# Head of a two-layer hybrid decoder step in a new order: filler products on TensorE, later powers, norms pair by pair

## The chip, the cores and the metric

One core of a Trainium2 chip. The time is that of one execution of the whole program on the device, in microseconds (us), and the result is the median of several executions. The engines are PE (TensorE, the matrix engine), DVE (VectorE), ACT (ScalarE), POOL (GpSimd) and SP (SyncE, which here only starts DMAs). They run side by side, each through its own instruction list, and meet through semaphores.

## The reference

Two layers over 256 prompt tokens and 64 sample tokens, 320 columns in all, 1024 features:

```python
for l in range(DEPTH):                                    # DEPTH = 2
    mod = silu(c) @ w_ada + b_ada                         # c: one prompt and 8 sample conditions
    shift, scale, gate = split(mod, 3)
    h = rms_norm(x, norm_g) * (1 + scale) + shift
    q, k, v, za, u, zs = split(h @ w_in)
    ya = attend(rope(q), rope(k), v, sinks)               # window 128
    ys, state = s5_branch(u, ...)                         # complex diagonal SSM, gelu, GLU
    x = x + gate * (concat(ya * silu(za), ys * silu(zs)) @ w_out)
y = rms_norm(x, final_g)
```

`s5_branch` needs, from small parameters only, `exp(a*dt)` with its sines and cosines, its powers 1 to 8 and B scaled by a coefficient. New key and value windows and SSM states are outputs too. All is float32.

## The kernel before, in words

Every engine's instruction list is written out by hand; nothing is scheduled by a planner. Activations lie feature by token: `xT`, eight tiles of 128x320. A dense product with a 1024x128 block of weights is made in three passes of float32r, `h_hi*w_hi + h_lo*w_hi + h_hi*w_lo`: ACT copies the block to `w_hi` (`hi_part`), DVE subtracts for `w_lo` (`lo_part`), and two buffers of each (`HL = 2`) are in use by turns. `DENSE` lists the blocks: u0 to u3, q0 to q3, k, v, za, zs, glu, out. PE's `project` makes 16 products of the high part and then 8 of the low part; `project_two` does u0 and u1 tile by tile, since it follows the tiles of `h` as they come.

**The head (layer 0).** SP starts the loads: condition, 16 half-megabyte blocks of `w_ada` (ss0 to ss15), small parameters, `ssm_b`, u0 and u1 and the rest. PE turns the condition, then x (eight tiles `xT0` to `xT7`); ACT squares each tile (`first_rows`, L1223), DVE copies it (L1619), and sums of squares go through `first_squares` and `newton` to `rstd`, which `spread_root` lays over all rows (`rb`). `modulation(0, "ssN")` multiplies block N with the condition: 2 products of 512 columns that use a quarter of the array's columns each. After four blocks ACT copies the sum (`modulation_rows`, L1288), PE turns it (`turn_modulation`, L798), and DVE adds it up to shift and scale (`modulation_of`, L1718 to L1726). Blocks 0 to 7 give shift and scale for tiles 0 to 3 of `h`, blocks 8 to 15 those for tiles 4 to 7. For a pair of tiles ACT scales and shifts the prompt's columns (L1323), DVE the samples' (L1899, L1902), ACT rounds to `h_hi` (L1328) and DVE subtracts for `h_lo` (L1906).

Between these lies the preparation of the SSM: DVE makes the angles and denominators (L1664 to L1679), ACT one Exp and two Sin (L1264, L1257, L1258), DVE the first power and the coefficient (`powers`), then `higher_powers`, `inputs_scaled` (B), `wide_powers`, and four times `turned_inputs`, whose results PE turns (`turn_B`, L862, placed by `TURNED_AFTER`). `lo_part(0, 2)` to `lo_part(0, 5)` stand among these on DVE, and `lo_part(0, 6)`, for q2, behind `outputs_summed` and `carriers(0, 0)`.

**The boundary.** While layer 0's out0 to out7 are added to x, ACT squares each tile into one of two buffers `sq`, DVE adds the first seven to `sqsum` (`add_square`), and PE sums over rows (`sum_squares`). At the start of layer 1 DVE scales tiles 0 to 3 by `rb` (`normed`, L1871) before the first pair, and 4 to 7 before the third.

PSUM's eight banks are three rings (`proj` 2 banks, `ada` 1, `work` 5), and a job of a ring waits until the job before it in its bank is read.

## Time and profile before

| | |
|---|---|
| median of 3 runs | 403.86 us (399.94 to 405.77) |
| profiled execution, time | 400.8 us |
| its span | 399.0 us |
| mean granted clock of TensorE | 0.97 of full speed |
| PE, DVE, ACT, POOL busy | 359.9, 316.1, 197.2, 64.8 us |
| DMA | 72.27 MB, mean 181 GB/s |

Times in rows are microseconds from the span's start. A row of the timeline has start, duration (from the first start to the last end where several are merged), engine, line, operation, `out<-in`, rows and columns, the count of records, and in brackets how long the engine sat idle before it and what it waited for.
### The profile page before, as it was taken

The page shows a single profiled execution, that of the slowest core. Times are in us where ns is not written, and L with a number is a line of the kernel's source. Part 1 is how long each engine was busy: PE and PEld are TensorE (multiplying, and loading weights), DVE is VectorE, ACT ScalarE, POOL GpSimd, SP SyncE. Part 2 cuts the span into 40 slices and gives each one's busy share as a digit, 9 for nine tenths or more (in the row PEclk, how much of TensorE's full clock was granted, in tenths as well). Part 3 has the DMA queues.
Part 4 walks back from the last instruction along what each step waited for, and adds up shares of the span by engine and source line. Part 5 has one row for each costly group of instructions (what it writes and reads, how often), then busy time and mean ns, then how long its engine had stood idle before and what let it go on. Part 6 is the DMA issues. An engine that isn't in the chain of part 4 may idle for free. (4 is left out here: it accounts for less than half of the span.)

```text
span 399.0 us, 8243 instructions
## 1 busy us (share of the span) xinstructions
PE 359.9 (90%) x3122; PEld 313.2 (79%) x3122; DVE 316.1 (79%) x676; ACT 197.2 (49%) x423; POOL 64.8 (16%) x58
## 2 busy tenths in 40 slices
PE   0997589998999799999999759999999999899993
PEld 0462379987979597977989758999997988779992
DVE  1648889977899958898599876889699589976863
ACT  2365255365463117787335556427633177863432
POOL 3200000020000370000499800000000000002430
PEclk9999969999999899999999959999999999999998
DMA  8999826799839966953995072391998279522303
GB/s 247 292 349 369 203 60 229 244 169 204 264 101 267 268 176 168 352 125 92 294 301 103 2 235 67 91 167 46 287 176 214 45 202 334 142 64 59 100 2 131
DMA packets 125125, 72.27 MB, mean 181 GB/s; under 512 B 63385, under 2 KB 111605, under 8 KB 124990
## 3 DMA queue, kind: packets, MB, share of 16 engines
q1 hardware_dynamic: 111118, 65.05, 61.3%
q10 hardware_dynamic: 13968, 6.69, 7.3%
q8 instruction: 25, 0.41, 0.4%
q14 instruction: 14, 0.11, 0.1%
HBM read 64.74 MB, written 6.59 MB: 179 GB/s over the span
## 5 line engine op out<-in xcount | busy, mean ns | idle before, releaser
L691 PE MATMUL bank<-h_hi,w_hi 128*128 128x320 f32 x448 | 138.6, 322 | 13.0 <-DVE h_lo L1906 10.7
L691 PE MATMUL bank<-h_lo,w_hi 128*128 128x320 f32 x448 | 134.4, 312 | 0.0
L691 PEld LDWEIGHTS bank<-h_hi,w_hi 128*128 128x128 f32 x448 | 85.6, 191 | 21.0 <-issue 12.4
L691 PEld LDWEIGHTS bank<-h_lo,w_hi 128*128 128x128 f32 x448 | 85.7, 191 | 0.2
L691 PE MATMUL bank<-h_hi,w_lo 128*128 128x320 f32 x448 | 81.8, 312 | 0.0
L1702 DVE TENSOR_TENSOR w_lo<-raw,w_hi 128x1024 fp32r<-128x1024 f32 x50 | 63.0, 1259 | 10.7 <-ACT w_hi L1272 10.4
L691 PEld LDWEIGHTS bank<-h_hi,w_lo 128*128 128x128 f32 x448 | 70.9, 191 | 0.0
L1272 ACT ACTIVATE w_hi<-raw 128x1024 fp32r<-128x1024 f32 x50 | 52.7, 1053 | 31.0 <-DMA raw<-in_w_in 16.9
L2304 POOL TENSOR_TENSOR ga<-xT,fing 128x320 f32<-128x320 f32 x4 | 6.5, 1632 | 141.8 <-DVE xT L2185 141.8
L1452 ACT ACTIVATE R<-R,sm 128x128 f32<-128x128 f32 (+2 forms) x40 | 17.7, 443 | 9.6 <-issue 5.7
L691 PE MATMUL bank<-R,Gm 128*128 128x96 f32 x128 | 17.4, 297 | 3.8 <-DVE R L2039 3.8
L691 PEld LDWEIGHTS bank<-R,Gm 128*128 128x128 f32 x128 | 16.4, 209 | 4.4 <-DVE R L2039 4.2
L691 PE MATMUL bank<-R,cT 128*32 128x512 f32 x136 | 19.1, 613 | 0.0
L1567 ACT ACTIVATE ez<-xT 128x320 f32<-128x320 f32 x16 | 7.6, 472 | 22.8 <-DVE xT L2185 22.8
L1353 ACT ACTIVATE hn<-bank 128x320 f32<-128x320 f32 x12 | 5.3, 438 | 27.5 <-PE bank L691 14.5
L691 PE MATMUL bank<-U,R 128*128 128x96 f32 x128 | 14.9, 276 | 1.4 <-DMA U<-u_turn 1.0
L691 PEld LDWEIGHTS bank<-U,R 128*128 128x128 f32 x128 | 14.6, 192 | 1.9 <-DMA U<-u_turn 1.3
L2054 DVE TENSOR_TENSOR R<-bank,const 128x512 f32<-128x512 f32 (+1 forms) x16 | 9.7, 650 | 8.0 <-PE bank L691 8.0
L1412 ACT ACTIVATE ez<-bank 128x320 f32<-128x320 f32 x16 | 6.9, 431 | 15.6 <-PE bank L691 11.4
L1462 ACT ACTIVATE HY<-bank 128x320 f32<-128x320 f32 x8 | 3.4, 438 | 19.9 <-PE bank L691 19.7
L1650 DVE TENSOR_TENSOR sqsum<-sqsum,ez 128x320 f32<-128x320 f32 x12 | 12.9, 1073 | 0.0
L2289 POOL TENSOR_TENSOR R<-Asd,Bbar 128x512 f32<-128x512 f32 x4 | 5.3, 1316 | 45.7 <-DVE h_lo L2174 45.5
(321 smaller groups left out, 638.1 us busy)
## 6 DMA issues: line engine op xcount, KB each, us to landing
R<-in_w_ada SPq DMA_DIRECT2D x34, 512.0 KB, 6.6
raw<-in_w_in SPq DMA_DIRECT2D x32, 256.0 KB, 5.9
raw<-in_w_in SPq DMA_DIRECT2D x14, 512.0 KB, 6.2
raw<-in_w_out SPq DMA_DIRECT2D x32, 128.0 KB, 3.6
raw<-in_w_out SPq DMA_DIRECT2D x16, 256.0 KB, 4.0
raw<-in_w_ada SPq DMA_DIRECT2D x4, 512.0 KB, 8.2
R<-in_w_in SPq DMA_DIRECT2D x4, 512.0 KB, 11.4
raw<-in_w_glu SPq DMA_DIRECT2D x4, 512.0 KB, 4.4
```

What stands on the lines that cost most here:

```text
L691: return nc.tensor.matmul(out_, lhsT, rhs, start=start, stop=stop, skip_group_check=free)
L1272: fn(w_hi[:, n % HL, :], place(l, unit), ACT.Copy).then_inc(hi_done, 1)
L1353: fn(qraw[:, n % 2, :], proj.bank(l, job)[:, 0:TOK], ACT.Copy).then_inc(proj.emptied(l, job), 1)
L1412: fn(ez[:, n % 2, :], proj.bank(l, job)[:, 0:TOK], ACT.Tanh, scale=0.5).then_inc(gate_tanh, 1)
L1452: fn(buf[:, v, i, :], buf[:, v, i, :], ACT.Exp, scale=SCALE, bias=sm[:, g, 1, x:x + 1], accum_out=sm[:, g, 2, x:x + 1])
L1462: fn(Ysb[:, 8 * n:8 * n + 8, :].rearrange("p (q h) j -> p q (h j)", h=2), src, ACT.Copy)\
L1567: fn(sq[:, m % 2, :], xT[:, m, :], ACT.Square).then_inc(sq_done, 1)
L1650: tt(sqsum[:, :], sqsum[:, :], sq[:, n % 2, :], ALU.add).then_inc(sq_added, 1)
L1702: tt(w_lo[:, n % HL, :], place(l, unit), w_hi[:, n % HL, :].bitcast(F32), ALU.subtract)\
L2054: tt(dst, src, mask, ALU.add).then_inc(work.emptied(l, job), 1)
L2289: step.add(tt(im, A(Asd[:, 0]), B(Bbar[:, 0]), ALU.mult))
L2304: tt(xn(k), xT[:, k, :], fing[:, k:k + 1].to_broadcast([P, TOK]), ALU.mult).then_inc(yn_ready, 1)
```

## The change

- **Filler.** A new helper `stay_busy(bank, n, cols)` multiplies the constant tile `mean` with itself into a bank that is written anew afterwards: 12 such products of 128 columns before the condition is turned, 5 between that and x.
- **Loads.** The small parameters go ahead of ss0 and ss1. `ssm_b` goes behind ss11, u0 and u1 behind ss7.
- **PE in the head.** `turn_inputs_B` goes from behind the squares to behind `project_two`, and into the ring `work`. The tiles of `project_two` come ahead: the pair 0, 1 stands ahead of ss8 and the pair 2, 3 ahead of ss10, where they stood behind ss11 and ss13.
- **DVE in the head.** Denominators behind `newton`; angles and `powers` behind tiles 0 to 3 of `h`; `higher_powers` behind tile 7; `wide_powers` behind the last `turned_inputs`. A third pair sum of squares on DVE saves a third of the products in `first_squares`.
- **ACT in the head.** Both copies of the modulation ahead of `hi_part(0, 0)`; the Exp joins the Sins, behind the third copy; `inputs_B` behind u0.
- **After u3.** `TURNED_AFTER` puts WB0 and WB1 behind u3, WB2 and WB3 behind q0, WB4 and WB5 behind q1, WB6 and WB7 behind q2.
- **Boundary.** The sixth addition to `sqsum` is gone, and PE multiplies the tiles 6 and 7 from both `sq` buffers (12 products for 8, here and at the end). `normed` goes pair by pair.

On PE, between the squares and the first products of u0 and u1, before (`qT`, `kcT`, `Toep`, `R` hold ss4 to ss7, `pt` and `scan` ss8 and ss9, `Gm` ss10 to ss12; L798 turns a modulation):

```order
L691 MATMUL bank<-kcT,cT 32x512 x2
L798 MATMUL bank<-const,R 128x128 x4
L691 MATMUL bank<-Toep,cT 32x512 x2
L691 MATMUL bank<-R,cT 32x512 x2
L798 MATMUL bank<-const,R 128x128 x4
L691 MATMUL bank<-pt,cT 32x512 x2
L691 MATMUL bank<-scan,cT 32x512 x2
L691 MATMUL bank<-Gm,cT 32x512 x4
L691 MATMUL bank<-h_hi,w_hi 128x320
```

And now, at the same place:

```order
L689 MATMUL bank<-qT,cT 32x512 x2
L689 MATMUL bank<-const,rstd 128x128 x2
L689 MATMUL bank<-const,rstd 128x64
L805 MATMUL bank<-const,R 128x128 x4
L689 MATMUL bank<-kcT,cT 32x512 x2
L689 MATMUL bank<-Toep,cT 32x512 x2
L689 MATMUL bank<-R,cT 32x512 x2
L805 MATMUL bank<-const,R 128x128 x4
L689 MATMUL bank<-h_hi,w_hi 128x320
```

Behind the second turned modulation comes `h` at once, and the blocks ss8 to ss11 stand behind the twelve products that follow.

On ACT, from the copy of the second modulation to the last pair of `h`, before (L1288 copies a modulation, L1257 and L1258 are the Sins):

```order
L1257 ACT_TABLE_LOAD
L1257 ACTIVATE HY<-HY 128x32
L1258 ACTIVATE HY<-HY 128x32
L1272 ACTIVATE w_hi<-R 128x1024
L1288 ACTIVATE R<-bank 128x512
L1272 ACTIVATE w_hi<-R 128x1024
L1323 ACTIVATE hf<-ga,mod 128x256 x2
L1328 ACTIVATE h_hi<-hf 128x320 x2
```

And now, around the third and fourth copy of a modulation (L1293):

```order
L1333 ACTIVATE h_hi<-hf 128x320 x2
L1293 ACTIVATE R<-bank 128x512
L1264 ACT_TABLE_LOAD
L1264 ACTIVATE HY<-HY 128x32
L1265 ACT_TABLE_LOAD
L1265 ACTIVATE HY<-HY 128x32
L1266 ACTIVATE HY<-HY 128x32
L1293 ACTIVATE R<-bank 128x512
L1328 ACTIVATE hf<-gs,mod 128x256 x2
```

The sines have moved from in front of the first pair of `h` to between the second and the third, with one more table load.

On DVE, from the last pair of `h` on, before (L1802 begins `inputs_scaled`):

```order
L1899 TENSOR_TENSOR hf<-gs,mod 128x64 x2
L1902 TENSOR_TENSOR hf<-hf,mod 128x64 x2
L1906 TENSOR_TENSOR h_lo<-hf,h_hi 128x320 x2
L1802 TENSOR_TENSOR scan<-Bsb,coef 128x256
L1803 TENSOR_TENSOR scan<-Bsb,coef 128x256
L1804 TENSOR_TENSOR Bbar<-scan 128x256
```

And now (L1778 to L1784 are `higher_powers`, 21 instructions):

```order
L1915 TENSOR_TENSOR hf<-gs,mod 128x64 x2
L1918 TENSOR_TENSOR hf<-hf,mod 128x64 x2
L1922 TENSOR_TENSOR h_lo<-hf,h_hi 128x320 x2
L1778 TENSOR_TENSOR HY<-Apow 128x32
L1779 TENSOR_TENSOR HY<-Apow 128x32
L1780 TENSOR_TENSOR Apow<-HY 128x2x16
```

The powers stand between the last tile of `h` and all that prepares u2 to q2.

The core of the diff:

```diff
-TURNED_AFTER = ({"u3": (0, 1, 2, 3), "q0": (4, 5), "q1": (6,), "q2": (7,)},
+TURNED_AFTER = ({"u3": (0, 1), "q0": (2, 3), "q1": (4, 5), "q2": (6, 7)},
...
@@ SP
-            for m in range(2):
-                load(0, f"ss{m}")
             for name, r0, r1 in (("norm_g", R_G, R_BADA), ("b_ada", R_BADA, R_BGLU), ("b_glu", R_BGLU, R_D)):
...
-            for m in range(2, 6):
+            for m in range(8):
+                load(0, f"ss{m}")
+            sp.wait_ge(*work.ready(0, "cT"))
+            load(0, "u0")
+            load(0, "u1")
+            for m in range(8, 12):
                 load(0, f"ss{m}")
             for r, name in enumerate(("ssm_b_re", "ssm_b_im")):
...
@@ PE
+            def stay_busy(bank, n, cols=512):
+
+                for _ in range(n):
+                    mm(bank[:, 0:cols], mean[:, :], (const if cols > P else mean)[:, 0:cols], True, True)
+
+            pe.wait_ge(mean_set, 1)
+            b = work.bank(0, "cT")
+            stay_busy(b, 12, P)
             pe.wait_ge(const_in, 16)
             pe.wait_ge(silu_r, 1)
...
+            stay_busy(work.bank(0, "xT0"), 5, P)
             pe.wait_ge(x_in, 32)
...
                     mm(o, sqsum[:, toks], mean[:, 0:1], True, False)
-                    mm(o, xn(4)[:, toks], mean[:, 0:1], False, False)
-                    ins = mm(o, xn(6)[:, toks], mean[:, 0:1], False, True)
+                    ins = mm(o, xn(4)[:, toks], mean[:, 0:1], False, True)
...
                     mm(o, sqsum[:, toks], mean[:, 0:1], True, False)
+                    mm(o, sq[:, 0, toks], mean[:, 0:1], False, False)
                     ins = mm(o, sq[:, 1, toks], mean[:, 0:1], False, True)
...
                     first_squares()
-                    turn_inputs_B()
-                    for m in range(2, 4):
+                    for m in range(2, 5):
                         modulation(0, f"ss{m}")
                     spread_root(0)
-                    for m in range(4, 8):
+                    turn_modulation(0, 0)
+                    for m in range(5, 8):
                         modulation(0, f"ss{m}")
-                        if m == 5:
-                            turn_modulation(0, 0)
                     turn_modulation(0, 1)
-                    for m in range(8, 12):
-                        modulation(0, f"ss{m}")
                     project_two(0, ("u0", "u1"), range(2), True)
-                    turn_modulation(0, 2)
-                    for m in range(12, 14):
+                    for m in range(8, 10):
                         modulation(0, f"ss{m}")
                     project_two(0, ("u0", "u1"), range(2, 4), True)
-                    for m in range(14, 16):
+                    for m in range(10, 12):
+                        modulation(0, f"ss{m}")
+                    turn_modulation(0, 2)
+                    for m in range(12, 16):
                         modulation(0, f"ss{m}")
                     turn_modulation(0, 3)
                     project_two(0, ("u0", "u1"), range(4, KT), False)
+                    turn_inputs_B()
                     turn_inputs_C()
...
@@ ACT
                 if l == 0:
-                    inputs_B()
                     modulation_rows(0, 0)
-                    ssm_sines()
+                    modulation_rows(0, 1)
                     hi_part(0, 0)
-                    modulation_rows(0, 1)
                     hi_part(0, 1)
                 for pair in range(0, KT, 2):
-                    if l == 0 and pair in (2, 4):
-                        modulation_rows(0, 2 if pair == 2 else 3)
+                    if l == 0 and pair == 4:
+                        modulation_rows(0, 2)
+                        ssm_sines()
+                        modulation_rows(0, 3)
...
@@ DVE
                 if l == 0:
-                    powers()
+                    denominators()
...
-                else:
-                    normed(range(4))
                 for pair in range(0, KT, 2):
-                    if pair == 4:
+                    if l:
+                        normed((pair, pair + 1))
+                    elif pair == 4:
+                        angles()
                         normed(range(4, KT))
                         if l == 0:
-                            higher_powers()
+                            powers()
                             modulation_of(0, 2)
                             modulation_of(0, 3)
...
                 if l == 0:
+                    higher_powers()
+                    lo_part(0, 2)
                     inputs_scaled()
+                    for m in range(4):
+                        if m:
+                            lo_part(0, m + 2)
+                        turned_inputs(m)
                     wide_powers()
-                    for m in range(4):
-                        lo_part(0, m + 2)
-                        turned_inputs(m)
...
-                    if m:
+                    if 0 < m < KT - 1:
                         add_square(m - 1, (l + 1) * KT + m)
```

## Rows read from the trace of the kernel before

**Rows 1.** The page: TensorE's granted clock in 40 equal slices, in tenths.
```profile
PEclk9999969999999899999999959999999999999998
```

**Rows 2.** The chain that ended last, in order of time: start, us, what.
```profile
242.40 0.50 DVE h_lo L1906
...
389.59 1.39 PE bank L691 x16
```

**Rows 3.** Timeline of PE in the head.
```profile
6.06 0.99 PE L698 MATMUL bank<-const,R 9*128 9x9 f32 x8 [6.06 <-DVE R L1613]
9.99 3.73 PE L713 MATMUL bank<-const,R 128*128 128x128 f32 x12 [2.94 <-DMA R<-in_x_sample]
...
17.60 1.93 PE L691 MATMUL bank<-raw,cT 128*32 128x512 f32 x8
...
23.08 2.04 PE L723 MATMUL bank<-const,R 64*128 64x64 f32 x16
...
26.92 1.84 PE L691 MATMUL bank<-const,rstd 128*128 128x128 f32 x6
...
35.75 1.04 PE L691 MATMUL bank<-Gm,cT 128*32 128x512 f32 x8
38.73 0.38 PE L691 MATMUL bank<-h_hi,w_hi 128*128 128x320 f32 x1 [1.94 <-DVE h_lo L1906]
...
51.01 0.64 PE L691 MATMUL bank<-h_hi,w_hi 128*128 128x320 f32 x1 [4.51 <-DVE h_lo L1906]
...
57.99 3.71 PE L691 MATMUL bank<-const,Gm 128*64 128x128 f32 x64
```

**Rows 4.** Busy us (and records) of stretches, then PEclk, DMA share, GB/s.
```profile
50.70:54.10 3.40, 2.73 (x9) 2.33 (x10) 2.66 (x10) 2.01 (x5) 0.00 (x0) 0.50 0.16 27
...
136.00:139.40 3.40, 3.40 (x18) 3.40 (x18) 3.33 (x5) 0.60 (x2) 3.24 (x5) 0.51 1.13 337
```

**Rows 5.** Timeline of DVE, head and the stretch behind it.
```profile
29.37 0.22 DVE L1739 TENSOR_TENSOR Apow<-HY 128x32 f32<-128x32 f32 x1 [3.94 <-ACT HY L1258]
...
31.94 1.68 DVE L1871 TENSOR_TENSOR ga<-xT,bank 128x320 f32<-128x320 f32 x4
...
42.67 0.22 DVE L1763 TENSOR_TENSOR HY<-Apow 128x32 f32<-128x32 f32 x1
...
47.73 0.31 DVE L1718 TENSOR_REDUCE mod<-bank 128x36 f32<-128x144 f32 x1
...
53.60 0.42 DVE L1802 TENSOR_TENSOR scan<-Bsb,coef 128x256 f32<-128x256 f32 x1
...
82.19 1.23 DVE L1702 TENSOR_TENSOR w_lo<-raw,w_hi 128x1024 fp32r<-128x1024 f32 x1
```

**Rows 6.** Timeline of ACT in the head.
```profile
27.70 1.28 ACT L1257 ACT_TABLE_LOAD   x1
28.99 0.23 ACT L1257 ACTIVATE HY<-HY 128x32 f32<-128x32 f32 x1
...
33.63 0.60 ACT L1288 ACTIVATE R<-bank 128x512 f32<-128x512 f32 x1 [3.34 <-PE bank L691]
34.12 1.05 ACT L1272 ACTIVATE w_hi<-R 128x1024 fp32r<-128x1024 f32 x1
```

**Rows 7.** DMA of ss15: its issue on SP's timeline.
```profile
27.40 0.48 SPq L530 DMA_DIRECT2D u_sb<-in_w_ada  x1
```

**Rows 8.** DMA issues: count, KB each, us to landing.
```profile
u_sb<-in_w_ada SPq DMA_DIRECT2D x1, 512.0 KB, 11.1
```

**Rows 9.** Timeline of PE, later in layer 0.
```profile
84.10 1.34 PE L691 MATMUL bank<-h_hi,w_lo 128*128 128x320 f32 x8
...
130.96 1.71 PE L691 MATMUL bank<-kT,qT 64*128 64x128 f32 x16
135.58 5.44 PE L691 MATMUL bank<-R,Gm 128*128 128x96 f32 x32 [2.91 <-DVE R L2039]
```

**Rows 10.** Timeline of DVE at the start of layer 1.
```profile
231.91 1.68 DVE L1871 TENSOR_TENSOR ga<-xT,bank 128x320 f32<-128x320 f32 x4 [1.93 <-PE bank L691]
```

More of the change, by code:

```diff
@@ L643, in _ @@
                     .then_inc(b_in, 16)
-            for m in range(6, 8):
-                load(0, f"ss{m}")
-            sp.wait_ge(*work.ready(0, "cT"))
-            load(0, "u0")
-            load(0, "u1")
-            for m in range(8, 16):
+            for m in range(12, 16):
                 load(0, f"ss{m}")
```

73 lines of the change are left out of this document (40 added, 33 removed).

## The prediction

> **What bounds the kernel now.** I read the page first, for where PE stands still and for its clock, then the chain of waits, then PE's timeline in the head, and last DVE's and ACT's at the same times. The page shows a clock near full speed but for four dips [rows 1], and from its busy shares PE as the main engine. The chain shows how much of this change can count: its tail passes through the last `h_lo` of layer 1 and the 16 records of the last sum of squares [rows 2]. So both boundary edits stand on the path, and what the head gains must come through PE to the end of layer 0.
>
> In the head PE has two losses. Equal products, four of 512 columns, take 1.93 us at 17.60 and 1.04 us at 35.75 [rows 3]: in the head the clock is at its lower level (1.2 GHz), and from some 34 us on at 2.4 GHz. And PE waits for `h`: 1.94 us before the first pair, 4.51 us before the third, and after this idle its 320-column products start at 0.64 us where they started at 0.38: the lower level again [rows 3], granted 0.50 in that stretch though PE is busy for 2.73 of 3.4 us [rows 4]. Behind the head PE hardly waits. One place matters: q2's low pass starts at 84.10 [rows 9], and DVE's `w_lo` for it ends at 82.19 + 1.23 = 83.4 [rows 5]. DVE is only 0.7 us ahead there.
>
> **Filler.** Eight products of 128 columns take 1.71 us late in layer 0, at the upper level [rows 9]: 0.21 each, so 0.43 at the lower. The other near row has three for 1.84 us at the lower level [rows 3], 0.61 each. Twelve cost 5.1 to 7.4 us from 1.0 on. I take 5.1, since constant tiles are nearer to the first row: they end at 6.2, and the condition, turned at 6.06 before [rows 3], loses nothing. It ends at 7.2, five more end at 9.4. x was there at 9.99 with a megabyte of ss0 and ss1 queued beside it [rows 3]; now it comes earlier. So x starts at 9.4, and at 12.9 by the dearer price.
>
> Their gain is the clock. What the profile shows of a rise is mixed: products of 96 columns without a gap run from 135.58, the stretch 136.0 to 139.4 still stands at 0.51, and the slices behind it are full again [rows 1, 4, 9]; but 7.6 us of turned x from 9.99 on brought none [rows 3]. The Trainium skill (TensorE: Matmul & The Clock Gate, "What's actually happening") says that the default state is throttled and that activity releases it. By that rule alone the turned x would have released it too; in this trace it did not, and the measurement decides. The filler is like what ran before the rise at 139.4, not like turned tiles, so I take it that it lifts the clock.
>
> **To the first pair of h.** Before, x takes 9.99 to 17.60 and the rest to the second modulation's copy lasts until 33.63 [rows 3, 6]. At the upper level PE stops being the pace of x; ACT's and DVE's copies are. I take 6.7 us, between PE's half (3.8) and the old 7.6, near the upper end since DVE has a dozen small steps in between: the squares start at 16.1. Of the 16.0 us behind 17.60 the turn of B (2.04, [rows 3]) and a third of the squares (about 1.2) leave, and ss4 to ss7 in other groups cost about 1.6, as blocks that use the same quarter of columns can't run side by side: 14.4, at the upper level 7.2, less 1.0 for ss0 and ss1, which now fit under x. The copy of the second modulation is at 22.4 instead of 33.63. From there to the first product was 38.73 - 33.63 = 5.1; the first high part (1.05, [rows 6]) now stands behind this copy, so 6.15: the first pair at 28.6, ten earlier. ss7, u0 and u1 have landed by then, since `ssm_b` went behind them.
>
> **To the third pair.** PE now has nothing between 23.5 and 28.6, where ss8 to ss11 stood. As behind the 4.51 us, I expect the lower level afterwards. Twenty-four products of h took from 51.01 to 57.99 less 0.4 of waiting, nearly all at the lower level, 6.5 us, and four blocks take twice 1.86: 10.2, or 5.3 at the upper level with twice 0.95 [rows 3]. The level comes back on the way, and I take the middle, 7.8: ss11 is done at 36.4. Then a chain that was spread out before: ACT's copy (0.6), two table loads of 1.28 and three small ones of 0.23 [rows 6], together 3.9 with the steps between: 40.3. DVE's `powers`, 31.94 - 29.37 = 2.6 [rows 5]: 42.9. From the start of the two last modulations to the end of the last pair 53.60 - 47.73 = 5.9 [rows 5]: 48.8. **The last pair ends at 48.8 instead of 53.6: 4.8 earlier.** Loads would allow 46.2: ss15 lands at 27.40 + 11.1 = 38.5 [rows 7, 8], plus product, copy and turn (about 2.2), one reduction less (0.4) and 5.9. By ACT's own row the next step starts 0.01 us after a table load [rows 6]; the Trainium skill (ScalarE: Activation LUTs, "What ACT_TABLE_LOAD costs") adds a drain and comes to 2.66 us each. With it the last pair would end 2.8 us later. The row shows none, so it stays out.
>
> **Where the gain goes.** `higher_powers` cost 47.73 - 42.67 = 5.1 us on DVE, and stood where PE waited for ss15 anyway. Now they stand behind the last pair, ahead of everything that feeds u2 to q2. `wide_powers` only changes its place within that stretch. So from the last pair to the part for q2 DVE needs 82.19 - 53.60 + 5.1 = 33.7 us: 48.8 + 33.7 = 82.5, ready at 83.7. PE would be there at about 79.9 (84.10 less 4.8, plus 1.0 for B's turn and less 0.4 for a turned tile that comes later); it waits 4 us and goes on at 83.7. **The 4.8 has become 0.4.** The later places of `TURNED_AFTER` spare PE a wait for the turned B, not this one. q3 and k follow one behind another from there; the scan on DVE, for which PE waits 2.91 at 135.58 [rows 9], has no free time to catch up, so the 0.4 stays.
>
> **Boundary and tail.** The chain's last sum of squares is 16 records in 1.39 us [rows 2]; with 24 it is 0.6 longer, and the addition saved ran beside ACT's last square: +0.6 at the end. At the first boundary copies on ACT cover it. Pair by pair the first tiles come 0.8 earlier (half of 1.68, [rows 10]), but DVE is the pace from 231.91 to 242.40 [rows 2, 10] and does the same work: +0.2. The new idle of 4 us before q2's low pass can cost clock: behind the 2.91 a stretch of 3.4 us stood at 0.51 [rows 4], 1.7 us; at three in ten that is +0.5.
>
> Sum: -0.4 + 0.6 + 0.2 + 0.5 = +0.9 on the profiled 400.8, so 401.7. The median of the runs shown is 3.1 above the profiled one; I put the forecast 0.4 under that offset, since one of its dips, behind 135.58, may fall otherwise: **404.3 us**.
>
> **Rivals.**
> - *The clock stays low in the head* (slower). If twelve fillers do not raise it, x ends at 17.0, squares at 21.4, the second copy is at 31.5 and the first pair at 37.7. Now ss8 to ss11 stand behind it, where they were done before: ss11 at 45.6, and the same chain of 12.4 gives 58.0 for the last pair: 4.4 later than before, with 5.1 of powers still behind. That is 9.2 above my case: 413.5. It decides where the level at the first modulation blocks is still that of 1.93 us for four products. For it: in the whole head before, it took until some 34 us. Against it: what ran ahead of the rise at 139.4 was such a stretch.
> - *The clock rises, and falls again at the squares*, for whose last sum PE waits after ss0 and ss1 as it now runs ahead of DVE: half of that, 407 to 410.
> - *The chain behind ss11 is covered.* If the clock holds over the gap before h, ss11 is at 33.9 and the last pair at the loads' 46.3: 2.5 less, 401.8; with waits that go elsewhere 399 to 402. Against it is the fall behind 4.51 us.
> - *More than that*, below 395.8, would need DVE to have spare time before q2; the 0.7 us speak against it.
> - *The gain doesn't arise at all* because loads bound the head: then the first pair stays near 38 while the clock is up; it ends near the second rival.
>
> The Trainium skill's same section on the clock makes idle time what throttles. By that rule the change works against itself, as it opens the gap before h; the fall behind the 4.51 us agrees, and the first case already carries it.
>
> **How the numbers follow.** Main case 0.48 (402 to 406.5), low clock 0.17, rise and fall 0.17, covered chain 0.14, more 0.04. The second case takes in loads that bound the head. The range leaves out the farthest gain and the top of the low-clock case, whose fillers could cost 3.5 more: 399.5 to 414. Two in a hundred, 8.1 us, is about what a measurement here tells from nothing: faster only in the last case and a bit of the one before, 0.05; slower in most of the low-clock case, 0.14; within, 0.81.
>
> **What would show it.** Right: four 512-column products near 1.0 us at ss0; a first pair of h near 28.6 and the last one's end near 49; two table loads before `powers`; PE idle some 4 us ahead of q2's low pass, put down to DVE's `w_lo`; 24 records at the end. Wrong: 1.9 us for those four products, or no idle before q2.

## The result and the profile after

The changed kernel takes **415.0 us** (median of 4, 413.3 to 420.8), the kernel before in the same session 402.8 (399.9 to 405.8): ratio 1.029, interval 1.018 to 1.040. Timed again with 6 executions it gave 414.9 and 1.031 (1.026 to 1.036). It is some 12 us slower, where 404.3 was forecast. The ratios leave out executions more than 1.5% above the fastest of their kernel; where over half of them lie there (`sinks_copy_early`, `changed_busy`), I go by the median of all.

The profiled execution is 413.5 us with a span of 411.7 and a mean granted clock of 0.929 (before: 400.8, 399.0, 0.970). The page's clock row, against [rows 1], has become restless in the first fifth:

```profile
PEclk9878779989999698999999869999998899999996
```

PE's timeline in the head, after:

```profile
1.06 4.67 PE L689 MATMUL bank<-mean 128*128 128x128 f32 x24 [1.06 <-DVE epsb L1615]
6.03 0.63 PE L703 MATMUL bank<-const,R 9*128 9x9 f32 x8 [0.29 <-DVE R L1620]
6.58 1.38 PE L689 MATMUL bank<-mean 128*128 128x128 f32 x10
8.57 2.35 PE L719 MATMUL bank<-const,R 128*128 128x128 f32 x12 [0.60 <-DMA R<-in_x_sample]
...
13.30 1.06 PE L689 MATMUL bank<-raw,cT 128*32 128x512 f32 x8
15.78 0.35 PE L689 MATMUL bank<-mean,sqsum 128*128 128x1 f32 x2 [1.42 <-DVE gs L1649]
...
17.07 1.06 PE L689 MATMUL bank<-raw,cT 128*32 128x512 f32 x8
18.88 1.92 PE L689 MATMUL bank<-qT,cT 128*32 128x512 f32 x4 [0.74 <-ACT R L1293]
...
26.95 0.66 PE L805 MATMUL bank<-const,R 128*128 128x128 f32 x4 [0.70 <-ACT R L1293]
32.63 0.60 PE L689 MATMUL bank<-h_hi,w_hi 128*128 128x320 f32 x1 [5.02 <-DVE h_lo L1922]
...
49.61 0.64 PE L689 MATMUL bank<-h_hi,w_hi 128*128 128x320 f32 x1 [4.69 <-DVE h_lo L1922]
...
82.01 2.50 PE L689 MATMUL bank<-R,cT 128*32 128x512 f32 x16 [3.63 <-DVE small L1935]
```

Read it by the price of equal work. Four products of 512 columns (x8) take 1.06 us at 13.30 and 17.07: the filler did lift the clock to 2.4 GHz, where [rows 3] had 1.93 us. At 18.88 two such products (x4) take 1.92: the level has fallen to 1.2 GHz, behind the wait of 1.42 us and the one-column products. So the first pair of `h` comes at 32.63. Windows over the stretches show the level (columns: busy time of PE, its weight loads, DVE, ACT and POOL, granted clock, DMA share, GB/s):

```profile
5.80:15.00 9.20, 7.74 (x52) 4.76 (x52) 5.32 (x16) 4.64 (x10) 2.67 (x3) 1.00 1.01 349
18.50:25.00 6.50, 6.12 (x22) 2.72 (x24) 2.73 (x9) 0.33 (x1) 0.00 (x0) 0.50 1.09 380
25.30:31.80 6.50, 1.61 (x12) 0.46 (x6) 3.61 (x9) 3.90 (x6) 0.95 (x1) 1.00 1.04 293
46.00:55.50 9.50, 5.76 (x20) 5.36 (x21) 7.67 (x35) 5.01 (x10) 0.00 (x0) 0.50 0.52 98
83.40:86.40 3.00, 3.00 (x14) 1.46 (x7) 2.93 (x5) 0.08 (x1) 1.62 (x2) 0.50 1.53 137
315.50:321.90 6.40, 6.40 (x31) 6.40 (x32) 6.30 (x11) 0.00 (x0) 0.00 (x0) 0.50 0.01 3
```

Note the second and third row: PE works for 6.12 of 6.5 us at 1.2 GHz, and idles for most of the next stretch at 2.4. The level follows what went before. DVE's timeline, against [rows 5]:

```profile
43.76 0.22 DVE L1754 TENSOR_TENSOR Apow<-HY 128x32 f32<-128x32 f32 x1 [4.24 <-ACT HY L1266]
...
51.16 0.89 DVE L1922 TENSOR_TENSOR h_lo<-hf,h_hi 128x320 fp32r<-128x320 f32 x2 [0.48 <-ACT h_hi L1333]
51.97 0.21 DVE L1778 TENSOR_TENSOR HY<-Apow 128x32 f32<-128x32 f32 x1
...
59.14 0.43 DVE L1817 TENSOR_TENSOR scan<-Bsb,coef 128x256 f32<-128x256 f32 x1 [0.90 <-ACT Bsb L1239]
...
81.80 0.15 DVE L1935 COPY small<-bank 128x4 f32<-128x4 f32 x1
...
86.53 2.36 DVE L1717 TENSOR_TENSOR w_lo<-raw,w_hi 128x1024 fp32r<-128x1024 f32 x2
```

The last pair ends at 52.05, 1.6 earlier than before; `w_lo` for q2 starts at 86.53 instead of 82.19, 4.3 later. Matching equal PE records of the two traces one by one shows where the end moved. The last column is after less before:

| place (PE) | before | after | difference |
|---|---|---|---|
| a product of u0 and u1, fourth pair | 55.11 | 53.47 | -1.6 |
| first product of u2 | 61.95 | 62.30 | +0.35 |
| first modulation of layer 1 | 78.83 | 82.01 | +3.2 |
| state products, layer 0 | 92.14 | 96.65 | +4.5 |
| products of the carried states (`R,Gm`), layer 0, record 22 of 64 | 139.63 | 143.94 | +4.3 |
| squares of layer 0, the second products with `sqsum` | 226.72 | 232.78 | +6.1 |
| carried states, layer 1, first record | 306.69 | 315.29 | +8.6 |
| carried states, layer 1, last of the first 32 records | 310.23 | 322.01 | +11.8 |
| last squares, the products of 64 columns | 390.54 | 402.96 | +12.4 |

Three places: the head (4.5), the scan of layer 1 (some 5, a wait of 2.62 us for 0.92 and 6.8 us at the lower level behind it), and bits between. The two rows of the scan, before and after:

```profile
306.69 3.81 PE L691 MATMUL bank<-R,Gm 128*128 128x96 f32 x32 [0.92 <-DVE R L2039]
```

```profile
315.29 7.06 PE L689 MATMUL bank<-R,Gm 128*128 128x96 f32 x32 [2.62 <-DVE R L2058]
```

The execution profiled before took 400.8 us where the median is 403.9. Matched in the same way against a second profile of that program (before_again below, span 404.1), the changed kernel is 2.7 us behind in the second half of the state products (3.9 there against the first profile) and only 1.8 behind just before the scan of layer 1 (6.8), and the scan costs 5.0 again. So the scan's part stands in both comparisons, while 5 of the 6.8 us in front of it are no more than two executions of one program differ by.

The chain of waits shows the scan's part, and the tail with 24 records where [rows 2] had 16:

```profile
295.33 0.60 SPq L536
295.98 8.29 DMA raw<-in_w_in
304.28 1.07 ACT w_hi L1277
305.38 1.23 DVE w_lo L1717
...
315.29 19.25 PE bank L689 x365
...
401.56 2.07 PE bank L689 x24
```

A weight load takes 8.29 us to land, ACT's `w_hi` waits for it, and DVE's `w_lo` and scan behind it.

### The profile page after: what moved, and what is told of

It reads as the page before. It is cut to its first block and busy times, and to the rows that moved or that the text cites. A ratio compares the mean times of both kernels' runs of the same rounds, so it can differ in the third digit from the quotient of the medians.

```text
span 411.7 us, 8326 instructions
## 1 busy us (share of the span) xinstructions
PE 370.9 (90%) x3164; PEld 325.5 (79%) x3164; DVE 315.2 (77%) x675; ACT 199.0 (48%) x424; POOL 64.7 (16%) x58
## 5 line engine op out<-in xcount | busy, mean ns | idle before, releaser
L689 PE MATMUL bank<-h_hi,w_hi 128*128 128x320 f32 x448 | 140.5, 326 | 16.0 <-DVE h_lo L1922 13.8
L689 PE MATMUL bank<-h_lo,w_hi 128*128 128x320 f32 x448 | 135.8, 315 | 0.0
L689 PEld LDWEIGHTS bank<-h_hi,w_hi 128*128 128x128 f32 x448 | 87.0, 194 | 23.7 <-issue 13.6
L689 PEld LDWEIGHTS bank<-h_lo,w_hi 128*128 128x128 f32 x448 | 87.2, 195 | 0.2
L689 PE MATMUL bank<-R,Gm 128*128 128x96 f32 x128 | 21.5, 343 | 5.5 <-DVE R L2058 5.5
L689 PEld LDWEIGHTS bank<-R,Gm 128*128 128x128 f32 x128 | 20.5, 254 | 6.1 <-DVE R L2058 5.9
L1360 ACT ACTIVATE hn<-bank 128x320 f32<-128x320 f32 x12 | 5.3, 438 | 28.7 <-PE bank L689 19.8
L2258 POOL MEMSET R<- 64x1280 f32 x4 | 4.6, 1160 | 58.4 <-PE bank L689 58.2
L689 PEld LDWEIGHTS bank<-R,cT 128*32 128x32 f32 x136 | 3.9, 110 | 12.5 <-issue 7.1
```

The lines of the kernel that those rows point to most:

```text
L689: return nc.tensor.matmul(out_, lhsT, rhs, start=start, stop=stop, skip_group_check=free)
L1360: fn(qraw[:, n % 2, :], proj.bank(l, job)[:, 0:TOK], ACT.Copy).then_inc(proj.emptied(l, job), 1)
L2258: nc.gpsimd.memset(Hblk[h * NST:(h + 1) * NST, :, :, 1 - h, :], 0.0).then_inc(hblk_zero, 1)
```

## The experiments

Eighteen kernels. Each was timed in turn with the kernel before; "of all" is the plain median of this kernel, "ratio" its time over that of the kernel before. The two do not always give the same difference, and where that matters both are given. The last four columns are from each one's profile: start of the first product of `h`, end of the last `h_lo` of layer 0, start of `w_lo` for q2, and PE's wait for R at the scan of layer 1.

| kernel | of all | ratio | interval | first h | last pair | w_lo q2 | R wait |
|---|---|---|---|---|---|---|---|
| before | 403.9 | | | 38.7 | 53.7 | 82.2 | 0.92 |
| before_again | 403.6 | 0.998 | 0.995-1.001 | 39.8 | 54.7 | 83.3 | 0.88 |
| changed_again | 414.9 | 1.031 | 1.026-1.036 | 33.6 | 54.5 | 88.3 | 2.67 |
| sinks_copy_early | 416.5 | 1.024 | 1.015-1.033 | 34.4 | 54.0 | 89.4 | 2.69 |
| boundary_of_before | 412.4 | 1.024 | 1.019-1.028 | 33.9 | 53.6 | 88.2 | 1.89 |
| boundary_alone | 406.3 | 1.008 | 1.004-1.011 | 38.2 | 53.2 | 81.7 | 1.12 |
| powers_early | 412.6 | 1.017 | 1.012-1.021 | 35.2 | 53.0 | 87.3 | 2.65 |
| higher_powers_back | 420.6 | 1.036 | 1.031-1.041 | 34.3 | 60.2 | 94.7 | 2.59 |
| changed_no_filler | 414.3 | 1.025 | 1.021-1.029 | 36.5 | 57.3 | 91.0 | 1.83 |
| before_with_filler | 407.4 | 1.009 | 1.005-1.012 | 38.4 | 53.4 | 81.9 | 2.62 |
| skews_late | 409.6 | 1.013 | 1.010-1.016 | 32.0 | 52.9 | 86.7 | 1.04 |
| all_early | 406.6 | 1.011 | 1.006-1.016 | 34.4 | 55.4 | 83.9 | 2.64 |
| all_early_no_fill | 406.7 | 1.006 | 1.004-1.009 | 36.4 | 57.8 | 86.3 | 1.03 |
| tiny_filler | 405.5 | 1.004 | 0.999-1.008 | 38.7 | 53.7 | 82.2 | 1.69 |
| before_skews_late | 402.2 | 0.993 | 0.990-0.996 | 38.6 | 53.5 | 82.0 | 0.94 |
| best_fill | 404.6 | 0.998 | 0.993-1.002 | 34.8 | 55.4 | 83.9 | 1.54 |
| best_fill_ss | 405.0 | 1.000 | 0.996-1.004 | 33.9 | 54.2 | 82.7 | 0.89 |
| changed_busy | 409.9 | 1.005 | 0.999-1.010 | 29.4 | 47.5 | 81.6 | 2.49 |
| best_busy | 406.0 | 1.005 | 1.000-1.009 | 31.7 | 51.9 | 80.4 | 1.19 |

**Both kernels once more.** Nothing edited.

> The changed kernel, nothing edited, for a second profile. In the first profiled execution it was 12.7 us longer than the kernel before: matched record by record, 3.9 of them stand at 100 us, 5.4 come at the scan of layer 1 (a wait of 2.6 us for R instead of 0.9, then a stretch at the lower clock), 1.2 at a dip near 158, the rest at the boundary and the tail. Theory 'head': only the wait ahead of layer 1's first modulation and what follows to 100 us belong to the change with certainty; the dips at 158 and 315 fall by chance. Then this profile has the wait of 3.6 us at 82 again, but other dips later, and the median is some 407 to 411 (before 402.8). Rival 'whole': the change sets the later dips too, through the times at which DMA and DVE work falls; then the dip behind the scan of layer 1 is there again, and the median is 412 to 416.

> The kernel before, nothing edited, for a second profile. All kernels profiled so far but two show a wait of 1.8 to 2.7 us for R at the scan of layer 1 (near 313) and the lower clock behind it, worth some 3 to 5 us; the first profile of the kernel before has 0.92 there and no fall. Theory 'chance': that was a lucky execution (400.8 beside a median of 403.3 to 404.1), and this one shows 1.8 or more with a span of 401 to 403. Theory 'head': the old head keeps DVE and its loads ahead, the wait is 0.9 again, and the gap of some 3.8 us that the new head loses behind 100 us is real.

Measured: the wait of 3.61 us at 83.8 is back, and so is all the rest: 2.67 at the scan of layer 1, median 414.9. The kernel before has 0.88 at its scan in a second profile:

```profile
311.73 0.69 PE L691 MATMUL bank<-R,Gm 128*128 128x96 f32 x4 [0.88 <-DVE R L2039]
```

So "chance" is out for that wait, though not for all falls of the clock: before_again, with a span of 404.1, has one at 155.9 to 159.3 that the first profile of the same program lacks.

**The wait at 82.** DVE's copy moved two turned inputs earlier.

```diff
                         turned_inputs(m)
+                        if m == 1:
+                            dve.wait_ge(sinks_turned, 1)
+                            dve.wait_ge(sinks_in, 48)
+                            cp(small[:, :, S_SINKS:S_SINKS + KV], ...)
                     wide_powers()
-                    dve.wait_ge(sinks_turned, 1)
-                    ...
```

> The changed kernel with DVE's copy of the sinks put behind the second turned input instead of behind the fourth and the wide powers. Theory 'ring': PE waits 3.63 us at 82.01 for this copy, since the bank that it empties takes the first modulation of layer 1, and falls to the lower clock behind the wait. With the copy at about 73 the wait goes; the modulation starts at about 78.4. But q2's low pass still waits for its w_lo at 86.5 + 1.2, so the wait only moves there: 2.0 to 3.5 us shorter in total than the changed kernel. Rival 'DVE': the wait is that of DVE's whole backlog, and moves entirely to w_lo: within 1 us of the changed kernel, with a wait of 3 us or more in front of q2's low pass.

The copy starts at 72.4 and the modulation waits for nothing, but q2's low pass does:

```profile
80.38 1.92 PE L689 MATMUL bank<-R,cT 128*32 128x512 f32 x16
...
90.67 1.70 PE L689 MATMUL bank<-h_hi,w_lo 128*128 128x320 f32 x5 [4.42 <-DVE w_lo L1717]
```

The rival holds in its mechanism: the wait is DVE's backlog, and the bank is only where PE meets it first. The times (416.5 of all, ratio 1.024) do not tell whether a microsecond was won.

**The boundary, both ways.** Squares of all tiles added on DVE and 8 and 16 products again, `normed` over four tiles; and the kernel before with those edits alone.

> The changed kernel with both layer boundaries as they were: squares summed on DVE for all eight tiles, 8 and 16 products instead of 12 and 24, the first four tiles normed together. Matched record by record, the changed kernel loses 0.8 us between the squares and the second pair of h of layer 1 and 0.9 at the tail. Theory 'small': 1.7 us shorter than the changed kernel, in those two places. Rival 'the boundary carries over': the later start of layer 1's first pairs moves the scan of layer 1 and its dip as well: 5 us shorter or more.

> The kernel before with only the two boundary edits of the change (last two squares summed by products, tiles normed pair by pair in layer 1); its head is untouched. Theory 'small': 1.7 us longer than the kernel before, ratio 1.004. Rival 'the boundary carries over': 5 us or more, ratio 1.012 or above, with a longer wait for R at the scan of layer 1 than the 0.9 of the kernel before.

Both ways give 3.0 us (1.031 to 1.024; 1.008), between the two theories; by the medians it is 2.5 (414.9 to 412.4) and 3.0. Rows show 0.7 at the tail (2.07 us for 24 records, 1.39 for 16), and in boundary_alone an earlier first pair of layer 1 (PE waits 2.74 instead of 3.42) that the second gives back (0.84 instead of 0.07). Most of the rest stands at the scan of layer 1. In boundary_of_before the wait there is 1.89 us instead of 2.62 and the lower level lasts from 313.8 to 317.2, 3.4 us instead of 6.8:

```profile
313.17 5.44 PE L689 MATMUL bank<-R,Gm 128*128 128x96 f32 x32 [1.89 <-DVE R L2058]
```

In boundary_alone the wait is 0.2 longer (1.12), and PE stands for 0.92 us among the products with `Toep`, with nothing in the profile that it waits for:

```profile
318.37 0.26 PE L691 MATMUL bank<-U,Toep 128*32 128x40 f32 x3 [0.92 <-issue]
```

So the boundary does carry over to the scan, by some 1.4 us in each of the two. Each is one profile; why it does was not tested.

**Powers.** Back in front of the last modulations; then all of them in DVE's idle times.

```diff
 higher_powers_back                       powers_early
+  powers(); higher_powers()  (pair 4)    +  denominators(); angles()
-  higher_powers()  (behind tile 7)       +  powers()         (ahead of lo_part(0, 0))
                                          +  higher_powers()  (ahead of normed(4..7))
                                          +  ssm_sines()      (ACT, behind copy 0)
```

> The changed kernel with the higher powers ahead of the last two modulations, as in the kernel before. DVE's work up to w_lo of q2 is the same in sum, so theory 'backlog' has w_lo of q2 start at 86.5 within 0.7 us and the time within 2 us of the changed kernel, with PE waiting about 9.8 us ahead of the third pair of h (4.7 in the changed kernel) and some 3.6 less in front of the modulation of layer 1 only if PE is late itself. Rival 'place': to stand behind the last pair is what costs, and the time falls by 3 us or more.

> The changed kernel with all the powers taken out of DVE's backlog: the angles stand right behind the root, the sines on ACT between the first two modulation copies (ACT idles there for 7.5 us in the changed kernel), the powers ahead of w_lo of u0 (DVE idle for 3.1 us), the higher powers ahead of the last four normed tiles (DVE idle for 4.2 us). Theory 'backlog': what PE waits for from the sinks copy to q2's low pass is DVE's 34.6 us of work behind the last pair, 5.1 of it the higher powers. Without them w_lo of q2 starts at 80 to 81.5 instead of 86.53, the wait of 3.63 us at 82 and the lower clock behind it go, and the kernel is 4 to 7 us shorter than the changed one: 408 to 411. Rival 'clock': the level falls somewhere in the head or at a later wait whatever DVE does, and what is won at 100 us is lost in one or two more dips: 412 to 415.

With the higher powers back the last pair ends at 60.2 and `w_lo` of q2 starts at 94.7: 5.7 us worse by the medians (420.6 to 414.9), 2 by the ratios. I had taken DVE's work as a sum that order can't change, but what feeds u2 to q2 can't start ahead of u0's products, so all of the delay comes behind. With the powers early the 5.1 us leave DVE and `w_lo` of q2 comes no earlier (87.3): DVE waits instead. The kernel is 2.3 us faster by the medians all the same, with the profiled span as long as that of the changed kernel (411.7), so no row shows where. DVE's timeline in powers_early:

```profile
56.02 1.23 DVE L1717 TENSOR_TENSOR w_lo<-raw,w_hi 128x1024 fp32r<-128x1024 f32 x1 [3.08 <-ACT w_hi L1277]
59.88 0.42 DVE L1817 TENSOR_TENSOR scan<-Bsb,coef 128x256 f32<-128x256 f32 x1 [2.63 <-ACT Bsb L1239]
```

5.7 us of waiting for 5.1 us of work. The second wait is for B, which the change turns behind the last pair. A second delay stood under the first.

**Both delays taken away.** PE turns B behind the third modulation, DVE goes on from the last pair in the order of before; then with the boundaries of before and without filler.

```diff
+                    turn_inputs_B()            (PE, behind turn_modulation(0, 2))
-                    turn_inputs_B()            (PE, behind project_two)
+                        inputs_B()             (ACT, behind modulation_rows(0, 2))
+                    inputs_scaled()
+                    wide_powers()
+                        lo_part(0, m + 2)
```

> The changed kernel with the powers early as in powers_early, and besides B turned by PE behind the third modulation's turn instead of behind the last pair, ACT's copy of it ahead of the fourth modulation's, and DVE's order behind the last pair as in the kernel before (inputs scaled, wide powers, then w_lo and turned inputs in turn). powers_early saved the 5.1 us of higher powers, but DVE waited 3.1 us for w_hi of u2 and 2.6 for the turned B instead. Theory 'DVE backlog': now it waits for neither, w_lo of q2 starts 28.6 us behind the last pair as in the kernel before, near 81 instead of 87, PE's wait of 3.6 us at 82 goes with the fall of the clock behind it, the state products start at 91 to 93, and the kernel is 4 to 7 us shorter than the changed one: 408 to 411. Rival 'clock': 412 to 415, with other falls in place of the one removed.

> The kernel of all_early with the boundaries of the kernel before and without the 17 constant products: the changed head in its best form by what the runs showed so far (boundaries 2.5 to 3 us, filler 0.6 to 3.4). Theory 'sum': all_early's gain of 4 to 7 and another 3 to 4 give 404 to 407, level with the kernel before. Theory 'loads': as ss15 lands no earlier than in the kernel before, the last pair ends at 53 or later and nothing can be won by this order: 403 at best. Rival 'filler needed': the head without filler stays at the lower clock until 28 us, the last pair ends at 56 to 57, and w_lo of q2 at 85: 407 to 411.

`w_lo` of q2 starts 28.5 us behind the last pair (before: 28.5) and PE no longer waits at the modulation of layer 1:

```profile
79.35 1.92 PE L690 MATMUL bank<-R,cT 128*32 128x512 f32 x16
```

1.031 became 1.011: 8 us, the largest single item, and more than theory "backlog" had said. The last pair itself, at 55.4, is no earlier than before.

**Filler.** Left out of the changed kernel; added alone to the kernel before; added with one column and one row of the array (`mm(bank[0:1, 0:1], mean[:, 0:1], mean[:, 0:1], True, True)`).

> The changed kernel without the 17 constant products in front of x. Theory 'filler lifts the clock': four products of 512 columns at ss0 take 1.9 us again instead of 1.06, x is done no earlier, the first pair of h comes some 4 to 8 us later (37 to 41 instead of 32.6), and all behind it: 4 to 8 us longer than the changed kernel. Rival 'the filler buys nothing lasting': the clock rises later but then has fewer dips in the head, and the time stays within 2 us of the changed kernel.

> The kernel before with the 17 constant products and nothing else. Theory 'loads and DVE bound the old head': the blocks come early, but ss15 still lands at 38.5 and the last pair of h ends at 51.5 to 53.6 as before, so the time is within 2 us of 403.3. Rival 'gain': with x and the squares at the upper level everything to the last pair moves by some 4 us and q2's low pass by as much: 399 to 400. Rival 'dips': PE runs ahead of its loads, waits more, and the clock falls more often: 405 or more.

> The kernel before with 17 constant products of one column and one row of the array in place of the 17 of 128 columns: the same count of instructions at the same places, next to no work. Theory 'fetch': the 34 more instructions move the point at which PE's instructions are fetched during layer 1's Toep copies from 27.6 to 23.5 us behind the state products, the weight load then lands at 28.7 instead of 26.4, PE waits 2.6 us for R, and the time is 2 to 3.5 us over the kernel before, as with the full filler (3.4). Rival 'clock': only the early rise of the clock does it, so this kernel has a wait of 0.9 to 1.1 there and is within 1 us of the kernel before.

Without filler the last pair ends 3 to 5 us later, yet the whole is no slower (1.025 to 1.031). Alone it costs 3.4 us though it brings the state products 1.4 us forward. In the head of before_with_filler the level is up only from 4.8 to 11.7 us and falls while PE turns x; it is back at 32.1, where the kernel before has it from 33.5, so this kernel gets little of the clock. Up to 306 us the two traces differ by less than 2, and then

```profile
308.52 0.89 PE L691 MATMUL bank<-R,Gm 128*128 128x96 f32 x3 [2.62 <-DVE R L2047]
```

and the lower level until 315.4; at 310 it is 5 us late. The tiny one moves nothing in the head that counts (last pair 53.7, `w_lo` 82.2) and has 1.69 there. Its time is 1.6 us longer, about half, but the interval (0.999 to 1.008) takes in no change at all. As far as that one profile goes, something that neither the clock nor work explains comes in with 17 more products (34 records) on PE.

In the DMA view of 4 us around the late load, as far behind the state products in both, the changed kernel has a packet on q8 that before_again lacks. I take q8 for the queue of PE's instructions, since the tiny products, which change PE's list alone, move its fetch from 27.6 to 23.4 us behind the state products of layer 1. The lines give packets, megabytes and share of the time:

```profile
q1 hardware_dynamic: 2109, 0.54, 114.0%
q10 hardware_dynamic: 201, 0.10, 14.9%
q8 instruction: 1, 0.02, 2.1%
q14 instruction: 1, 0.01, 0.8%
```

```profile
q1 hardware_dynamic: 2492, 0.63, 92.4%
q10 hardware_dynamic: 215, 0.11, 17.4%
q14 instruction: 1, 0.01, 0.9%
```

On q1, which carries 65 of the program's 72 MB, fewer packets go in the changed kernel in these 4 us, and they take longer. Counted from the state products of layer 1, that fetch starts at 27.5 to 27.8 us in the three profiles of the kernel before and of boundary_alone, and the load lands at 26.3 to 26.5. In nine others with either filler and the Toep copies at their old places it starts at 23.4 to 24.2, and the load lands at 27.3 to 29.4. The Trainium skill (Runtime: NRT & Kernel Launch, "Instruction fetch mechanics") says that an engine's sequencer fetches its code in 16 KiB blocks over its own DMA queue, and that the cost is mostly hidden. The packets are of that size here. That the fetch among the Toep copies delays the load fits these twelve, but two do not fit: changed_no_filler has its fetch at 27.8 and the load at 27.5, with a wait of 1.83, and changed_busy fetches at 16.9 and 33.7 and has the load at 28.2 and a wait of 2.49. So the fetch is at most a part of it. What is shown is that the load lands late there in every kernel that has the filler or the changed head and the copies at their old places, but for all_early_no_fill (26.2); that the count of instructions alone brings some of it rests on the one profile of tiny_filler (27.3).

**The Toep copies.** All behind zs0 in layer 1, in the changed kernel and in the kernel before.

```diff
-           [None] * 2 + ["za2", "za2", "za3", "za3", "zs0", "zs0"])
+           [None] * 2 + ["zs0"] * (T - 2))
```

> The changed kernel with layer 1's skewed copies of Ksb into Toep all issued behind zs0, as in layer 0, instead of two by two behind za2, za3 and zs0. Theory 'queue': the wait of 2.6 us for R at 315 comes from ACT's w_hi, which waits 2.1 us for a weight load that SP issues behind the Toep copies (2.8 and 5.3 us of SP's time for four of them, 4.0 in the kernel before). Without them in front the wait for R falls to 0.9 or below, the fall of the clock behind it goes, and the kernel is 3 to 5 us shorter: 410 to 412. Rival 'Toep late': PE waits for Toep at 322 instead, by 2 us or more, and nothing is gained. Rival 'scan': the wait for R is the length of DVE's scan and stays at 2.6.

> The kernel before with layer 1's skewed copies all behind zs0. In the changed kernel this took 7 us away (1.031 to 1.013), the wait for R from 2.62 to 1.04 us and the fall of the clock behind it. Theory 'fetch': the kernel before has 0.9 there already, so it gains at most 1 us: ratio 0.998 to 1.000. Rival 'every kernel': a gain of 3 us or more here too, ratio 0.993 or below; then the Toep copies are a cost that has nothing to do with the change.

```profile
312.55 1.69 PE L689 MATMUL bank<-R,Gm 128*128 128x96 f32 x13 [1.04 <-DVE R L2058]
```

Theory "queue" holds: without the copies ahead of the weight load the wait falls to 1.04, the level stays up, and 7 us go by the ratios (1.031 to 1.013), 5.3 by the medians; between the two profiles it is 4.4, of which 3.9 arise from here on. PE does not wait for Toep. The kernel before gains 2 to 3 us as well, with its wait unchanged, so part of that gain has another source; this is the only kernel here that beats the one before (0.990 to 0.996).

**All mends together.**

> The kernel of all_early (powers and B early), with the boundaries of the kernel before and layer 1's skewed copies late; filler kept. By sums: all_early 1.011, less 3 us for the boundaries and 4 to 7 for the scan of layer 1, gives 397 to 401, ratio 0.982 to 0.995. Rival 'overlap': what the two mends win is partly the same dip, and the ratio is 0.996 to 1.004.

> The kernel of best_fill with modulation blocks ss8 to ss10 ahead of the first pair of h and ss11 ahead of the second, where PE otherwise idles 5.1 us. Theory 'gap': the wait before the first pair falls to some 2 us or less, the clock does not fall at 31, and the last pair comes 1 to 2 us earlier: 1 to 3 us below best_fill. Rival 'loads': ss8 to ss10 have not landed when PE gets there, the first pair comes later, and the time is that of best_fill or more.

0.998 and 1.000: rival "overlap" holds. The single gains (8, 3 and 7 us) would come to 18; together they give 13 by the ratios and 10 by the medians. In best_fill_ss the wait before the first pair falls from 5.08 to 3.24 and the last pair comes 1.2 earlier, but not the end.

**Constant products in PE's waits of the head.** 4 ahead of the squares, 18 ahead of the first pair, 14 ahead of the third (best_busy: 4, 11, 9).

```diff
+                stay_busy(work.bank(0, "rms"), 4, P)
+                    stay_busy(proj.bank(0, "u0"), 18, P)
+                    stay_busy(work.bank(0, "BT0"), 14, P)
```

> The changed kernel with constant products of 128 columns in PE's three waits of the head: 4 ahead of the squares (wait 1.42), 18 ahead of the first pair of h (5.02), 14 ahead of the third pair (4.69); 0.21 us each at the upper level, so 0.8, 3.8 and 3.0 us. Theory 'clock': the falls at 18, 32 and 46 go or get shorter, the first pair comes at 28.6 to 31 as predicted (32.0 to 33.6 in the changed kernel), the last pair ends at 48.8 to 51 (52.1 to 54.5), and the kernel is 1.5 to 4 us shorter than the changed one: 411 to 413.5. Rival 'chain': first and last pair are set by ACT's and DVE's copies and the loads, the last pair ends within 1 us of 52 and the time is within 1.5 us of 415. Rival 'cost': products at the lower level take 0.43 each, stretch beyond the waits and delay both pairs: 416 or more.

> The kernel of best_fill_ss with constant products in its waits: 4 ahead of the squares, 11 ahead of the first pair, 9 ahead of the third. Theory 'clock': the falls at 17 and 44 to 58 go, the last pair ends at 50 to 52 instead of 54.2, the state products start at 88 to 90 instead of 92.2, and the time is 400 to 402.5, ratio 0.990 to 0.996. Rival 'chain': the last pair stays at 53 to 54 and the time at 404 to 405.

PE's timeline in changed_busy:

```profile
18.50 1.05 PE L689 MATMUL bank<-qT,cT 128*32 128x512 f32 x4 [0.74 <-ACT R L1297]
...
24.18 4.18 PE L689 MATMUL bank<-mean 128*128 128x128 f32 x36
29.35 0.38 PE L689 MATMUL bank<-h_hi,w_hi 128*128 128x320 f32 x1 [0.99 <-DVE h_lo L1926]
...
45.06 0.42 PE L689 MATMUL bank<-h_hi,w_hi 128*128 128x320 f32 x1 [1.56 <-DVE h_lo L1926]
...
77.10 1.92 PE L689 MATMUL bank<-R,cT 128*32 128x512 f32 x16 [3.61 <-DVE small L1939]
```

Two products in 1.05 us at 18.50 instead of 1.92: the level holds from 6.8 to 47.8. The first pair comes at 29.35, the last ends at 47.5, and the median falls by 5. DVE's backlog is untouched: PE waits 3.61 at 77.10. Theory "clock" holds for the head, by more than it said. It fails in best_busy, whose last pair and `w_lo` come 2.3 us earlier than in best_fill_ss (51.9, 80.4) while the time stays at 406 (405 there). The level did not hold there either. PE does the same as in changed_busy up to 18 us, with 4 constant products ahead of the squares and a wait of 0.17, and still falls from 18.6 to 22.0:

```profile
18.73 1.92 PE L690 MATMUL bank<-qT,cT 128*32 128x512 f32 x4 [0.74 <-ACT R L1296]
```

So one profile in two shows that the 4 products keep the level up at the squares. And in powers_early the level falls at 15.5, just as the squares begin; their first two records take 0.56 us where the changed kernel has 0.35:

```profile
15.48 0.56 PE L689 MATMUL bank<-mean,sqsum 128*128 128x1 f32 x2 [1.42 <-DVE gs L1649]
```

So the fall does not need the one-column products. Ahead of it stand the turned tiles of x and the wait, and which of these counts no run separates.

## Why the prediction was wrong

**What held.** The filler ends at 5.73 (6.2 said), x starts at 8.57 (9.4), the squares at 15.78 (16.1), the four products of ss0 take 1.06. The chain behind the third modulation, from the end of ss11's products to the last pair's end, was put at 12.4 and is 12.1, counted from ACT's copy at 39.93. The table loads cost what their row says: 1.28 us at 40.54, the next step at 41.84; the drain of the Trainium skill (ScalarE: Activation LUTs, "What ACT_TABLE_LOAD costs") is not in this trace either. DVE needs 33.6 us from the last pair to `w_lo` of q2 when its wait of 0.9 is taken off; 33.7 was said. The tail grew by 0.7; 0.6 was said. One sum has a slip: by the dearer price of the filler x comes at 12.5 (1.0 + 7.4 + 1.0 + 3.1), not 12.9; the main case does not use it.

**First failure: "the rest ... at the upper level 7.2".** The clock was to stay up from the filler to the first pair. The level fell at the squares, the place of the second rival, and the second copy is at 26.30, not 22.4; the first pair 32.63, not 28.6; the last pair 52.05, not 48.8. changed_busy shows that this is the whole of it: with the level held, 29.4 and 47.5. The case got 0.17 and 407 to 410. I had the wait ahead of the squares in the rival's own words and did not ask what PE does before it: turned tiles of x, which had brought no rise in the kernel before either [rows 3]. The Trainium skill (TensorE: Matmul & The Clock Gate, "What's actually happening") has the clock set by how busy the engine has been recently. The trace agrees: the level falls in or behind all three waits of the head (1.42, 5.02 and 4.69 us). I used it for one gap only.

**Second failure: "The 4.8 has become 0.4".** It became +4.3: 1.6 earlier, 5.1 of higher powers, 0.9 for B. The first term is the clock's, the second was right. With the level held, in changed_busy, `w_lo` of q2 starts at 81.63, 0.6 earlier than before, where 0.4 was forecast; so with the level held the sum up to q2 would have come out. all_early takes the same delay away by the order alone. The third I had priced on PE (1.0) and not on DVE, which waits for the turned B. I also named the wrong instruction: PE waits 3.63 us at the first modulation of layer 1, whose bank of the ring `ada` holds the sinks that DVE has not read, not at q2's low pass. sinks_copy_early moved that wait to the named place with 4.42, so the sum was not hurt by it.

**Third failure: the boundary, +0.2 and +0.6.** Measured twice: 3.0. The tail's term is right. The prediction stopped the boundary's effect at the pairs of layer 1; the runs have some 1.4 us of it at the scan of layer 1.

**Fourth failure: a missing term.** The prediction stopped at q2. The filler was costed at nothing beyond the head, and alone it costs 3.4 us some 300 us later, at the scan of layer 1, behind a load that lands 2.2 us late (28.7 for 26.5); perhaps half of that comes with the count of instructions alone. In the changed kernel the load lands 2.4 late and the scan costs 5 us. skews_late takes 4 to 7 us away at this place. That this is outside the head shows in changed_busy: its head is as good as forecast, and its median is still 409.9. What exactly delays the load stays open.

In round numbers of the 12 us: the order of B and powers 8, the boundaries 3, the filler 1 to 3; and what comes at the scan of layer 1 some 5; they overlap, as best_fill shows. The gain of the early pairs was never cashed: all_early_no_fill ends its last pair at 57.8 and is as fast as all_early at 55.4.

## What to carry to other kernels

When work is moved off one chain, ask of each thing that it feeds what else that waits for: here the powers hid a late B, and only both together gave the time back. Filler lifts the clock only up to the next thin stretch; put it where the engine waits, or leave it out, and profile to the end of the program, since what is added in the first microseconds can cost in a crowded DMA stretch 300 us later. A reordering wants a run of each half by itself: 5 to 7 us here came out of DMA issues that the change never touched.

## What the runs showed of the hardware

- In ten profiles with the filler and the changed head, and no constant products in the waits, TensorE fell to 1.2 GHz between 15.5 and 18.4 us and stayed there for 7 to 14 us, although it had been at 2.4 GHz for 10 us or more before. Ahead of the fall stand turned tiles and a wait of 1.4 us. Constant products in three waits of the head (1.2, 4.2 and 3.3 us of work) kept it at 2.4 GHz for 41 us, from 6.8 to 47.8, in changed_busy; in best_busy it fell at 18.6 all the same.
- The spread of executions of one kernel goes in part with the clock: of the kernel before, 400.0 and 400.3 us had mean granted clocks of 0.961 and 0.965, 405.8 and 405.8 had 0.946 and 0.945. But other executions of it with 400.4 and 405.7 us had 0.952 and 0.953.
- A 256 KB weight load took 8.29 us to land among small Toep copies, and 5.2 in the same place of before_again.
